# Four norms lose their normalized rows and the banded attention's transposes become products with a diagonal matrix

## The reference, cut to what matters

```
def rmsnorm_2(x, g):
    y = x * rsqrt(mean(x * x, axis=-1) + EPS)
    return y * g
for l in range(2):
    h = rmsnorm_2(x, g_attn[l]);  proj = h @ w_in[l]     # 18 column tiles of 128
    qa, ka, va, qb, kb, vb = split(proj)
    # qa, ka, qb, kb: another rmsnorm per head, then rotary; va, vb as they are
    ya = windowed_gqa_sink(qa, ka, va, sink[l])  # |key - query| <= 128: a band of 2 or 3 key blocks
    yb = diff_attention(qb, kb, vb, lam)
    x = x + concat(ya, rmsnorm_2(yb, subln[l]) * c) @ w_out[l]
    h = rmsnorm_2(x, g_ffn[l]);  gate, val = split(h @ w_up[l])   # 44 column tiles
    gate = conv3_over_tokens(gate, conv_w[l], conv_b[l])
    x = x + (silu(gate) * val) @ w_down[l]
```

## Time and profile before

| | us |
|---|---|
| median of 3 runs | 3194.21 (3192.61 to 3195.34) |
| the profiled execution's own time | 3192.74 |
| its span | 3191.0 |
| PE busy | 2972.4 (93%) |
| DVE busy | 1523.6 (48%) |
| ACT busy | 1190.8 (37%) |
| mean granted clock of PE | 0.972 of full speed |

### The profile page before, as it was taken

The page is one execution under the profiler, slowest core; times in us unless marked ns, Lnnn a source line. Parts: engine busy times, 40 slices in busy tenths (PEclk is TensorE's granted clock), DMA queues, the critical chain, the costliest instruction groups (busy, mean ns, idle before and its releaser), DMA issues.

```text
span 3191.0 us, 36914 instructions
## 1 busy us (share of the span) xinstructions
PE 2972.4 (93%) x14632; PEld 2430.2 (76%) x14632; DVE 1523.6 (48%) x2217; ACT 1190.8 (37%) x1784; POOL 0.2 (0%) x4
## 2 busy tenths in 40 slices
PE   6999699999999889999999998789999997899999
PEld 4788588999999766557888776368888774478887
DVE  3121755552454444436636456855444457654343
ACT  3111543331332365334424344643233444543232
POOL 0000000000000000000000000000000000000000
PEclk9999899999999999999999999999999998999999
DMA  6665001221212111002322211012223220023223
GB/s 243 220 225 183 7 31 53 67 67 59 66 60 71 49 39 39 1 14 95 107 92 93 99 67 53 1 53 99 100 92 102 76 73 14 14 86 106 87 98 106
DMA packets 67276, 255.94 MB, mean 80 GB/s; under 512 B 7456, under 2 KB 11168, under 8 KB 66464
## 3 DMA queue, kind: packets, MB, share of 16 engines
q1 hardware_dynamic: 67104, 253.58, 23.1%
HBM read 251.46 MB, written 2.10 MB: 79 GB/s over the span
## 4 chain that ended last, share of the span: by engine, by line
PE 85%; DVE 6%; DMA 3%; ACT 3%; issue 3%; SPq 0%; DVEq 0%; ACTq 0%
PE psum L520 71%; DVE arena L1371 2%; ACT temps L1014 2%; DVE row_stats L1371 2%; DMA modulation_weights<-in_ada 2%; PE psum L837 2%; PE psum L856 1%; PE psum L834 1%; PE psum L559 1%; PE psum L977 1%; DMA arena<-in_ada_first 1%; PE psum L757 1%; PE psum L771 1%; PE psum L847 1%; DVE temps L1371 1%
## 5 line engine op out<-in xcount | busy, mean ns | idle before, releaser
L520 PE MATMUL psum<-arena_r,w_hi 128*128 128x512 f32 (+1 forms) x7640 | 2077.3, 371 | 42.3 <-DVE arena_r L1371 38.8
L520 PEld LDWEIGHTS psum<-arena_r,w_hi 128*128 128x128 f32 x7640 | 1404.0, 189 | 254.4 <-issue 78.0
L520 PE MATMUL psum<-arena_r,w_lo 128*128 128x512 f32 (+1 forms) x3820 | 1264.6, 367 | 0.0
L1371 DVE TENSOR_TENSOR w_lo<-w_raw,w_hi 128x1024 fp32r<-128x1024 f32 (+3 forms) x367 | 453.9, 1237 | 768.8 <-ACT w_hi L1014 768.7
L520 PEld LDWEIGHTS psum<-arena_r,w_lo 128*128 128x128 f32 x3820 | 709.4, 189 | 84.9
L1014 ACT ACTIVATE w_hi<-w_raw 128x1024 fp32r<-128x1024 f32 (+3 forms) x367 | 391.7, 1067 | 829.6 <-DMA w_raw<-in_weights 829.4
L1371 DVE SCALAR_TENSOR_TENSOR temps<-psum,vectors,temps 128x511 f32<-128x511 f32 x352 | 228.0, 679 | 150.4 <-ACT temps L1014 147.3
L1014 ACT ACTIVATE temps<-psum,vectors 128x512 f32<-128x512 f32 (+1 forms) x132 | 112.2, 850 | 179.8 <-PE psum L520 178.4
L1014 ACT ACTIVATE arena<-psum 128x768 f32<-128x768 f32 (+1 forms) x134 | 96.6, 727 | 155.3 <-PE psum L520 63.7
L1014 ACT ACTIVATE temps<-temps 128x512 f32<-128x512 f32 (+2 forms) x165 | 108.3, 656 | 90.6 <-DVE temps L1371 88.6
L1014 ACT ACTIVATE temps<-psum 128x512 f32<-128x512 f32 (+1 forms) x142 | 86.9, 655 | 145.6 <-PE psum L520 123.8
(11 more groups left out here) (147 smaller groups left out, 1850.9 us busy)
## 6 DMA issues: line engine op xcount, KB each, us to landing
w_raw<-in_weights SPq DMA_DIRECT2D x275, 512.0 KB, 3.2
w_raw<-in_weights SPq DMA_DIRECT2D x64, 704.0 KB, 4.0
temps<-in_ada SPq DMA_DIRECT2D x40, 512.0 KB, 3.6
modulation_weights<-in_ada SPq DMA_DIRECT2D x40, 512.0 KB, 4.4
arena<-in_ada_first SPq DMA_DIRECT2D x4, 2048.0 KB, 23.7
X<-in_xt SPq DMA_DIRECT2D x1, 3072.0 KB, 12.6
phase_constants<-in_const SPq DMA_DIRECT2D x3, 768.0 KB, 7.4
w_raw<-in_weights SPq DMA_DIRECT2D x12, 192.0 KB, 2.3
```

The costliest lines, as they stand in the source:

```text
L520: last = mm(lin_at(t, segs, slots, upper)[:, s:s + m], w[:, c], x(k, s, m), start=(k == 0 and a == 0), stop=(k == n_k - 1 and a == 2))
L1371: op(*args, **kw).then_inc(*C.out(signal))
```

## The change

For the four norms without shift (before the attention and before the FFN of both layers of the second block) the rows are no longer normalized before the projection. While the residual is written, ACT rounds X·g to a hi part (`raw_hi`) and DVE makes the lo part (`raw_low`), at a place of their own in the arena (RAW0). PE starts the first projection tile on them and issues the sums of the norm after k = 3 of that tile; from then on single tiles, no interleaved pair. ACT makes the factor rs from the sum (`factor`) into RS, a part of X that holds nothing any more. The factor is applied after the projection: DVE multiplies each projected attention tile out of PSUM (`raw_scaled`) before ACT takes it; in the FFN it multiplies each gate tile into SCALED before the convolution, and once more the product of silu and value. The banded attention leaves its exponentials undivided; DVE writes two 128x128 diagonal matrices with the reciprocals (SHARE), and `turn` multiplies by these instead of transposing.

```diff
+        RAW0 = 24576
+        RS = X[:, 0:2, NX:NT]
+        SCALED = [ADA_IN[:, 0:NX], ADA_IN[:, NX:2 * NX]]
+        SHARE = [T[:, n, 0:256].rearrange("p (h q) -> p h q", h=2) for n in range(2)]
 # PE: ffn(segs, raw)
+                if raw:
+                    linear(1, segs, hi, lo, "free_v", 4, progress("raw_done", 8), between=lambda k: norm_sum(segs) if k == 3 else None)
+                else:
+                    norm_sum(segs)
+                    linear(2, segs, hi, lo, "free_v", 4, progress("h_done", 8))
 # PE: attention of the second block
-                norm_sum(ONLY_X)
-                pe.wait_ge(*C.next("lam_in"))
-                mm(PS[:, 5, 0:2], ones, ST[:, 32:34], start=True, stop=True).then_inc(*C.out("lam_sum"))
-                ready = progress("h_done", 8)
+                def sums():
+                    norm_sum(ONLY_X)
+                    pe.wait_ge(*C.next("lam_in"))
+                    mm(PS[:, 5, 0:2], ones, ST[:, 32:34], start=True, stop=True).then_inc(*C.out("lam_sum"))
+                ready = progress("raw_done", 8)
...
-                        linear(2, ONLY_X, hi2, lo2, "free_a", 4, ready)
-                    elif n > 1:
-                        linear(1, ONLY_X, hi2, lo2, "free_a", 4)
+                        linear(1, ONLY_X, raw_hi, raw_lo, "free_a", 4, ready, between=lambda k: sums() if k == 3 else None)
+                    else:
+                        linear(1, ONLY_X, raw_hi, raw_lo, "free_a", 4)
 # PE: turn(n) of the banded attention
-                            last = pe.transpose(PS[:, hf, t * P:(t + 1) * P], f_(a, P), ident)
+                            last = mm(PS[:, hf, t * P:(t + 1) * P], f_(a, P), SHARE[n % 2][:, hf], start=True, stop=True)
 # ACT: factor, residual, ffn_up, pipeline
+            def factor():
+                load_set(LN_EXP_SET)
+                act.wait_ge(*C.next("sum_done"))
+                inverse_root(RS, halves(PS[:, 4, :]), D, "rs_made")
+                    if gain is not None:
+                        step(r_(RAW0 + m * NX, NX), X[:, m, 0:NX], ACT.Identity, "raw_hi", scale=gain(m), bias=v_("zero"))
...
+                                act.wait_ge(*C.next("raw_scaled"))
+                            step(T[:, part, 0:nt], SCALED[i % 2] if raw else lin_at(t, segs, 4), ACT.Identity, "u_made",
...
+                        if raw:
+                            act.wait_ge(*C.next("raw_scaled"))
+                            step(T[:, par, 0:nt], T[:, 2 + par, 0:nt], ACT.Square if sp_["kind"] == "norm" else ACT.Copy, "free_a")
 # DVE: residual, ffn_up, pipeline, probs
+            def raw_low(m, gain):
+                dve.wait_ge(*C.next("raw_hi"))
+                step(stt, "raw_done", r_(RAW0 + 8 * NX + m * NX, NX), X[:, m, 0:NX], gain(m), r_(RAW0 + m * NX, NX).bitcast(F32),
+                     ALU.mult, ALU.subtract)
...
+                        if raw and part == 0:
+                            dve.wait_ge(*C.at("lin_done"))
+                            src = SCALED[i % 2]
+                            step(tt, "raw_scaled", halves(src), halves(lin_at(t, segs, 4)), RS, ALU.mult)
...
+                    if raw:
+                        step(tt, "prod_made", halves(T[:, 3, 0:NX]), halves(T[:, 3, 0:NX]), RS, ALU.mult, after=C.at("free_v"))
...
+                    if raw and n < len(specs):
+                        dve.wait_ge(*C.at("lin_done"))
+                        step(tt, "raw_scaled", halves(T[:, 2 + n % 2, 0:NX]), halves(lin_at(t, ONLY_X, 4)), RS, ALU.mult,
+                             after=C.at("tail_made") if n >= 2 else None)
...
-                    step(tt, "p_made", e, e, ST[:, s + 12:s + 14].rearrange("p (h o) -> p h o", o=1).broadcast_to([P, 2, w]), ALU.mult,
-                         after=C.at("dve_own"))
+                    step(tt, "p_made", SHARE[n % 2], CF[:, C_ID:C_ID + P].rearrange("p (o q) -> p o q", o=1).broadcast_to([P, 2, P]),
+                         ST[:, s + 12:s + 14].rearrange("p (h o) -> p h o", o=1).broadcast_to([P, 2, P]), ALU.mult, after=C.at("dve_own"))
```

More of the change, by code:

```diff
@@ L1051, in norm, with residual @@
                         split_to(t + 2)
-            def residual(segs, squares):
+            def factor():
+                load_set(LN_EXP_SET)
+                act.wait_ge(*C.next("sum_done"))
+                inverse_root(RS, halves(PS[:, 4, :]), D, "rs_made")
+            def residual(segs, squares, gain=None):
                 nt, added = width(segs), C.n["sq_added"]
@@ L1072, in ffn_up @@
                 for i in range(FH):
+                    raw = kind == 2
                     for part in range(2):
@@ L1080, in ffn_up, with ffn @@
                     step(T[:, 2, 0:nt], T[:, 1 if kind == 1 else 0, 0:nt], ACT.Silu, "silu_made")
-                    if kind == 1:
+                    if kind == 1 or raw:
                         act.wait_ge(*C.next("prod_made"))
-                    else:
+                    if kind == 2:
                         act.wait_ge(*C.next("free_v"))
                     step(r_(ACT0 + i * nt, nt), T[:, 3, 0:nt], ACT.Copy, "act_hi")
-            def ffn(kind, l, segs, shift, last=False):
-                norm(segs, shift)
+            def ffn(kind, l, segs, shift, last=False, gain=None):
+                if kind == 1:
+                    norm(segs, shift)
+                else:
+                    factor()
                 load_set(SILU_SET)
@@ L1091, in ffn @@
                     ffn_up(kind, l, half, segs)
-                    residual(segs, half == 1 and not last)
+                    residual(segs, half == 1 and not last, gain if half == 1 else None)
             load_set(SILU_SET)
@@ L1359, in _ @@
                 outputs(3)
-                residual(ONLY_X, True)
-                ffn(2, l, ONLY_X, zero, last=l == 1)
+                residual(ONLY_X, True, lambda m: v_("g_ffn", l * 8 + m))
+                ffn(2, l, ONLY_X, None, last=l == 1, gain=None if l else lambda m: v_("g_attn", 8 + m))
         @block.vector
@@ L1416, in add_square, with residual @@
                 step(tt, "sq_added", SQSUM[:, 0:nt], SQSUM[:, 0:nt], T[:, 4 + m % 2, 0:nt], ALU.add, after=C.at("sq_added"))
-            def residual(segs, gate, squares, upper=0):
+            def residual(segs, gate, squares, upper=0, gain=None):
                 nt = width(segs)
@@ L1428, in residual, with conv @@
                         add_square(m - 1, nt)
+                    if gain is not None and m:
+                        raw_low(m - 1, gain)
                 if squares:
                     C.n["res_sq"] += 1
-            def conv(kind, l, half, i, part, segs, t):
+                if gain is not None:
+                    raw_low(7, gain)
+            def conv(kind, l, half, i, part, segs, src):
                 marks = []
@@ L1463, in ffn_up, with ffn @@
                          ALU.subtract)
-            def ffn(kind, l, segs, gain, shift, gate, last=False):
-                norm(segs, gain, shift)
+            def ffn(kind, l, segs, gain, shift, gate, last=False, next_gain=None):
+                if kind == 1:
+                    norm(segs, gain, shift)
+                else:
+                    dve.wait_ge(*C.next("rs_made"))
                 for half in range(2):
                     ffn_up(kind, l, half, segs)
-                    residual(segs, gate, half == 1 and not last)
+                    residual(segs, gate, half == 1 and not last, 0, next_gain if half == 1 else None)
             step(dve.memset, "zero_made", CS[:, :], 0.0)
@@ L1750, in _ @@
                     step(tt, "lam_in" if c else "dve_own", ST[:, 32 + c:33 + c], v_(f"lq{c + 1}", l), v_(f"lk{c + 1}", l), ALU.mult)
-                norm(ONLY_X, lambda k, s: v_("g_attn", l * 8 + k), zero)
+                dve.wait_ge(*C.next("rs_made"))
                 dve.wait_ge(*C.next("lam_exp"))
@@ L1835, in _ @@
                 low(3)
-                residual(ONLY_X, one, True, 4)
-                ffn(2, l, ONLY_X, lambda k, s: v_("g_ffn", l * 8 + k), zero, one, last=l == 1)
+                residual(ONLY_X, one, True, 4, lambda m: v_("g_ffn", l * 8 + m))
+                ffn(2, l, ONLY_X, None, None, one, last=l == 1, next_gain=None if l else lambda m: v_("g_attn", 8 + m))
 INPUTS = ("x c ctx c_ctx w_ada b_ada norm_mix norm_ffn gla_w_in gla_gate_w1 gla_gate_w2 gla_gate_b gla_out_norm "
```

51 lines of the change are left out of this document (26 added, 25 removed).

## The result

The changed kernel took 3153.74 us (median of 4 runs, 3149.05 to 3157.23) against 3194.78 (4 runs) before: a ratio of 0.9872, 95% interval 0.9857 to 0.9887. In a later comparison of 5 runs against 17 it took 3159.70 against 3192.90, 0.9895 (0.9879 to 0.9910). Taken together the intervals say faster by 0.9 to 1.4%. The prediction was 3160 with a range of 3148 to 3180. The profiled execution took 3157.23, its span 3155.4: 35.6 us less than the profiled span of before, where the prediction said 34.2.

What follows compares the result with a forecast made beforehand. PE was taken as the bound: 85% of the chain, 71% of the span in projection matmuls. Norms -33.0, projection-end wait +1.4, banded attention -2.6 make -34.2 us: 3192.74 to 3158.5, as a median 3160, range 3148 to 3180.

Steps and rivals of the forecast that it cites:

- The four norms: Between residual and next projection: gaps 30.4 and lost clock 9.9 us won, 6.9 and 0.4 of products kept, net 33.0.
- the forecast sum for their place: Per norm: the gap, its 0.17 us and the clock's loss, less products; -7.6 and -8.1 us at the two attentions.
- DVE's cover in the FFN: Added FFN multiplications, 61 us of DVE work, lie under PE: 6.8 of 10.98 us per pair of tiles, costing nothing.
- The wait at the end of the attention's projections: PE waits for the last value tile because raw_scaled comes ahead of ACT's copy: 0.7 us per layer, +1.4 in all.
- the wait of 1.03: Banded attention, one step of four: PE 0.76 us later and DVE 0.27 earlier, so DVE waits 1.03 us.
- +0.4 for the start: Banded attention's start, which goes once through PE with a p step before it: 0.4 us slower per layer.
- -1.5: Banded attention's drain if the busier PE keeps its clock: 1.5 us less; the other end was +1.7, 0 was taken.
- 2: Rival, banded attention: the whole DVE gain comes, -13 us instead of -2.6, giving 3150; chance 0.09.
- 3: Rival, norms: PE stands 1.5 us and the clock falls again (2.5 us), 16 us in all, giving 3176; chance 0.17.
- 4: Rival, FFN up tiles: DVE becomes the bound, every added operation on the path, 86 us, giving 3246; chance 0.03.
- 5: Rival, banded attention: the whole stage falls to half clock, +49 us, giving 3211; chance 0.05.
- 6: Rival, banded attention: a true product costs four times a transpose, +37 us in all, giving 3200; chance 0.02.

Runs made afterwards that it cites:

- e1: The changed kernel without its banded part (exponentials divided by DVE, blocks transposed as before): 3161.69 us, ratio 0.9903 to the kernel before.
- e7: The changed kernel plus four unread DVE multiplications per pair of FFN tiles, 121 us of DVE work: 3156.34 us, ratio 0.9891.
- e4: The changed kernel with PE's order in a banded attention step changed to turn, scores, values: 3154.42 us, ratio 0.9883.
- e5: The changed kernel with banded blocks transposed again, DVE writing only the diagonal matrices, division by row sums left out: 3148.48 us, ratio 0.9870.
- e6: The changed kernel with the four norms' sums asked after k = 0 of the first tile instead of k = 3: 3156.60 us, one time.
- e2: The kernel before with the banded part of the change alone (diagonal matrices and true products): 3185.81 us, ratio 0.9983.
- The fillers: Unread products of constants put at PE's waits in the diff attention: on e4 3140.39 us, ratio 0.9840; on the kernel before 3188.20 us, 0.9991.

## Why the prediction was right, and where it wasn't

**The total: in part luck.** Of the 35.6 us between the two profiles the norms gave 35.1 (forecast 33.0), the banded attention with its start 6.8 (1.2), and executions differed by 2.1 before the first norm; the diff attention took 8.3 back, which the forecast had at nothing. Without that loss the profiled execution would have come to about 3149, at the lower end of the range. The mechanism was right for the norms and the steps of the banded attention, not for the rest.

**The four norms: right.** Forecast 33.0, found 35.1 in the table of stages. PE doesn't stop, and the clock isn't lost. The sums stand in the stream at 0.86 us each. e1 shows that these parts are nearly all of the change: 0.9903 alone.

**A gain that I missed.** In both attention stages the norms gave 0.9 us more than the forecast sum for their place. The interleaved pair had a second price: both its tiles end together, and PE stood before the first tail product. Timeline of PE, before and changed:

```profile
2529.03 0.39 PE L520 MATMUL psum<-arena_r,w_lo 128*128 128x512 f32 x1
2529.91 1.12 PE L757 MATMUL psum<-temps,fixed_constants 128*128 128x512 f32 x2 [0.50 <-ACT temps L1014]
```

```profile
2502.61 0.39 PE L529 MATMUL psum<-arena_r,w_lo 128*128 128x512 f32 x1
2502.83 1.02 PE L771 MATMUL psum<-temps,fixed_constants 128*128 128x512 f32 x2
```

0.88 us from one to the next against 0.22. That is 0.7 of the 0.9.

**DVE's cover in the FFN: right, with room.** PE was busy for all of the window with DVE at 61% of it, and at 85% in e7. A pair holds 6.72 us of DVE work, where the prediction had 6.8. The 61 us of added work cost nothing.

**The wait at the end of the attention's projections: too small.** Forecast 0.7 per layer. From the last projection to the first mask it is 4.12 us against 2.87, 1.2 more: raw_scaled's 0.70, ACT's own wait behind it, and the first scores at 1.09 instead of 0.73 us: the granted clock of that stretch is 0.89, where it was 1.00.

**The banded attention: steps right, ends mis-sized.** Turn 1.60 (forecast 1.63), DVE's p step 0.43 (0.42), four steps 13.32 (13.3), the wait of 1.03 shown by e4. The sum around the steps was mis-sized. Less its start wait, the stage gained 4.5 us in layer 0, where the forecast was 1.3. From first mask to the end, the start gave 0.6 (the term "+0.4 for the start" had the wrong sign), the two full groups of four steps 1.2 as forecast, the three steps before the drain 1.3, and the drain's products 1.3 (5.29 us against 6.58), where the prediction took 0 and named -1.5 as the favourable end. The three steps got -0.45 in the sum, their share of a group's -0.6. But none of them is the step at which PE sets the time, so all of DVE's saving comes through: 0.54 + 0.54 + 0.27 us. The rule of the Trainium skill that the prediction set aside (TensorE: Matmul & The Clock Gate, Part 4: PE-mode transpose) points the way that the drain went: with transposes it had 0.58 before and 0.70 in e5, with products 1.00. The middle of e5 had 0.98 with transposes all the same, which the rule alone doesn't lead one to expect. These runs don't separate the kind of instruction from the longer time that PE is busy with it.

**Rivals.** 2: DVE's whole gain needs e4's order; then the banded stage gains 6.4 and 6.8 us over the kernel before. 3: didn't happen; a stop of 0.77 us at that place costs 1.0 (e6), where the rival put 4 on one of 1.5. 4: shown wrong (e7). 5: the opposite happened, 1.00 behind the first 16 us, which have 0.68 as before. 6: a true product costs 1.8 times a transpose (1.60 to 0.87).

**What wasn't in the prediction.** The diff attention. All that its forecast of no change rested on was that its code is the same. It takes 66.8 to 69.6 us in six layers of three profiles with the old banded part in front (before twice, e1), 71.0 to 71.1 in all six of the changed kernel and 69.5 and 70.9 in e2. The fillers show that the difference is PE's clock. PE waits there for up to 3.6 us at a time, alike in both kernels, and behind the same wait of 2.00 us the clock fell in one profile and not in the other. So PE's own work in the 14.6 us before it doesn't decide it. Why it falls there more often behind true products stays open: e5, with transposes in front, lies between at 68.7, and e6, with products, had 71.0 and 68.7.

## What to carry to other kernels

A factor per token commutes with a projection. Moving it behind the matmul pays when PE waits for the norm, and the price has to fit under PE: here 88 DVE operations did. Count the clock with each gap: behind the norms' gaps of 7.3 to 7.7 us PE lost 1.6 to 2.9 us more to it, behind a wait of 0.77 us nothing. In stages where PE waits in short turns, products that nobody reads can be worth more than the work they delay: 10.7 us here, and nothing that can be told in the kernel before.

## What I hadn't expected of the hardware

A stage whose code is untouched took 4.3 us more because PE's clock fell behind a wait of 2.00 us that was the same before, and it was then steady to 0.1 us over three executions. The kernel before, on the other hand, took 67.1 us in one execution and 69.6 in another for that stage in layer 1. Its time goes from 3183.78 to 3198.74 us over all comparisons, while its two profiled executions differ by 0.7 us, so most of that spread isn't in any profile here.
